# Who makes the sums of weight blocks in the gated layers' way down: VectorE, or an accumulating DMA issued by GpSimd

## The reference, cut to what matters

```
def swiglu(x, w_in, w_out):
    gate, up = jnp.split(x @ w_in, 2, axis=-1)     # w_in: 1024 x 5632
    return (jax.nn.silu(gate) * up) @ w_out        # w_out: 2816 x 1024
x = x + 0.5 * rms_norm(swiglu(rms_norm(x, ln_ffn1_pre[l]), w_ffn1_in[l], w_ffn1_out[l]), ln_ffn1_post[l])
```

## Time and profile before

| what | us |
|---|---|
| median of 3 runs | 2791.99 (2789.7 to 2792.78) |
| the profiled execution's own time | 2794.04 |
| its span, first to last instruction | 2792.3 |
| PE busy | 2722.2 (97% of the span) |
| DVE busy | 2006.4 (72%) |
| ACT busy | 1407.1 (50%) |
| POOL busy | 58.2 (2%) |
| mean of what the DMA engines moved | 94 GB/s |

### The profile page before, as it was taken

The page is one execution under the profiler, slowest core; times in us unless marked ns, Lnnn a source line. Parts: engine busy times, 40 slices in busy tenths (PEclk is TensorE's granted clock), DMA queues, the critical chain, the costliest instruction groups (busy, mean ns, idle before and its releaser), DMA issues. The chain is left out here.

```text
span 2792.3 us, 51093 instructions
## 1 busy us (share of the span) xinstructions
PE 2722.2 (97%) x21196; PEld 2405.1 (86%) x21196; DVE 2006.4 (72%) x2795; ACT 1407.1 (50%) x2154; POOL 58.2 (2%) x45
## 2 busy tenths in 40 slices
PE   8999999999999999999999999999999998999998
PEld 7999888778999878999888777999888877888877
DVE  7888855676887876887856777788785369666674
ACT  4445544555544455544545555444556367444442
POOL 1000000001000001000000000100000000000000
PEclk9999999999999999999999999999999999999999
DMA  4334311103233231334122103133422111322243
GB/s 150 107 106 174 104 49 61 40 4 121 85 106 132 110 136 46 99 106 176 62 86 76 55 3 114 61 107 106 159 96 101 62 51 35 114 82 94 96 166 106
DMA packets 72806, 261.26 MB, mean 94 GB/s; under 512 B 7864, under 2 KB 8888, under 8 KB 72576
## 3 DMA queue, kind: packets, MB, share of 16 engines
q1 hardware_dynamic: 72576, 257.99, 26.9%
HBM read 255.86 MB, written 2.10 MB: 92 GB/s over the span
## 5 line engine op out<-in xcount | busy, mean ns | idle before, releaser
L261 PE MATMUL ps<-h_hi,w_space 128*128 128x512 f32 (+1 forms) x2624 | 697.5, 351 | 3.4 <-DVE h_lo L367 3.4
L261 PEld LDWEIGHTS ps<-h_hi,w_space 128*128 128x128 f32 x2624 | 462.6, 190 | 70.5 <-DVE h_lo L367 4.2
L271 PE MATMUL ps<-w_space 128*128 128x512 f32 x2064 | 480.2, 391 | 1.7 <-DVE w_space L249 0.9
L249 DVE TENSOR_TENSOR w_space<-w_raw,w_space 128x1024 fp32r<-128x1024 f32 x252 | 307.1, 1230 | 214.6 <-ACT w_space L241 214.5
L261 PE MATMUL ps<-h_lo,w_space 128*128 128x512 f32 (+1 forms) x1312 | 457.4, 349 | 0.0
L271 PEld LDWEIGHTS ps<-w_space 128*128 128x128 f32 x2064 | 385.3, 188 | 81.8 <-DVE w_space L249 1.7
L848 PE MATMUL ps<-h_hi,w_space 128*128 128x256 f32 x2432 | 450.8, 283 | 0.0
L848 PEld LDWEIGHTS ps<-h_hi,w_space 128*128 128x128 f32 x2432 | 385.2, 192 | 0.2
L848 PE MATMUL ps<-h_lo,w_space 128*128 128x256 f32 x1216 | 344.3, 283 | 0.0
L241 ACT CAST w_space<-w_raw 128x1024 fp32r<-128x1024 f32 x252 | 261.0, 1047 | 159.5 <-PE ps L261 97.3
L261 PEld LDWEIGHTS ps<-h_lo,w_space 128*128 128x128 f32 x1312 | 249.4, 190 | 29.8 <-issue 0.5
(11 more groups left out here) (532 smaller groups left out, 3978.3 us busy)
## 6 DMA issues: line engine op xcount, KB each, us to landing
w_raw<-in_w_ffn_in SPq DMA_DIRECT2D x176, 512.0 KB, 3.4
w_raw<-in_w_in SPq DMA_DIRECT2D x64, 512.0 KB, 3.4
w_raw<-in_w_ffn_out SPq DMA_DIRECT2D x56, 512.0 KB, 3.5
w_raw<-in_w_up SPq DMA_DIRECT2D x44, 512.0 KB, 3.4
w_raw<-in_w_down SPq DMA_DIRECT2D x34, 512.0 KB, 4.1
row_blocks<-in_w_ffn_out SPq DMA_DIRECT2D x8, 2048.0 KB, 11.6
w_raw<-in_w_out SPq DMA_DIRECT2D x24, 512.0 KB, 4.3
w_raw<-in_w_ple_gate SPq DMA_DIRECT2D x16, 512.0 KB, 3.8
```

The lines of the kernel that those rows point to most:

```text
L249: nc.vector.tensor_tensor(self.shaped(unit, self.lo(n)), self.whole_of(unit), self.shaped(unit, self.hi(n)).bitcast(F32), ALU.subtract).th ...
L261: m = nc.tensor.matmul(c.ps[:, bank, t], part[:, cols], moving[:, k, t], start=(opens and k == 0 and i == 0), stop=(k == KD - 1 and i == 2 ...
L271: m = nc.tensor.matmul(c.ps[:, bank + half, :], x, part[:, half * S:(half + 1) * S], start=(first and i == 0), stop=(final and i == 2), sk ...
```

## The change

The four weight sums of each group are no longer made by DVE. POOL issues for each one a DMA that reads a block of `w_out` from HBM and adds it to the block that lies in SBUF (`accum_op=ALU.add`). Since such a DMA only adds, the signs of the scheme are turned: m5 uses b11+b12, m6 b11+b12+b22, m7 b12+b22, m4 b11+b12+b22+b21, and the activation sums and the joins of the products take the opposite signs where needed (same number, shapes and places of DVE instructions). ACT waits for the DMA's semaphore in place of DVE's. Beside that, in the attention that follows, five semaphores become two (`cos_done` and `sin_done` are `halves_done`; `summed` and `inverted` are `shared`), with the same waits in other counts.

```diff
     def waiting(self, name, g):
         def wait(eng):
             if name in SUMMED_WEIGHTS:
-                self.wait_rested(eng, "weights", name, g)
+                self.wait_weights(eng, name, g)
...
+    def wait_weights(self, eng, name, g):
+        eng.wait_ge(self.c.blocks_summed[g], 16 * (1 + len(SUMMED_WEIGHTS) * self.stage + SUMMED_WEIGHTS.index(name)))
...
     def vector_down(self, dve, nc, early, last):
         for k in range(4, UNITS):
             self.collect(dve, nc, k)
-            if k + 2 < UNITS and DOWN_STEPS[k + 2][0] in SUMMED_WEIGHTS:
-                self.weight_sum(dve, nc, *DOWN_STEPS[k + 2])
...
-    def weight_sum(self, dve, nc, name, g):
...
-        if name == "m5":
-            self.wait_blocks(dve, g)
-            nc.vector.tensor_tensor(b11, b12, b11, ALU.subtract).then_inc(done, 1)
...
+    def weight_sums(self, pool, nc):
+
+        for i, name in enumerate(SUMMED_WEIGHTS):
+            part, rows, half = {"m5": ("m1", 0, 1), "m6": ("m1", 2, 1), "m7": ("m7", 2, 1), "m4": ("m1", 2, 0)}[name]
+            before = {"m5": "m1", "m6": "m5", "m4": "m6"}.get(name)
+            for g in range(2):
+                if i:
+                    self.wait_weights(pool, SUMMED_WEIGHTS[i - 1], g)
+                else:
+                    self.wait_blocks(pool, g)
+                if before:
+                    pool.wait_ge(self.c.W.lo_ready, self.down.d0 + STEP_OF[before, g] + 1)
+                pool.dma_start(self.block_weights(part, g), self.w_blocks[g][:, rows:rows + 2, half * S:(half + 1) * S],
+                               accum_op=ALU.add).then_inc(self.c.blocks_summed[g], 16)
...
-            nc.vector.tensor_tensor(total, a21, a22, ALU.add).then_inc(done, 1)
+            nc.vector.tensor_tensor(total, a21, a22, ALU.subtract).then_inc(done, 1)
...
-            nc.vector.tensor_tensor(total, total, a11, ALU.subtract).then_inc(done, 1)
+            nc.vector.tensor_tensor(total, a11, total, ALU.subtract).then_inc(done, 1)
...
-            self.add_sums(dve, nc, "m1", "m5")
+            self.add_sums(dve, nc, "m5", "m5", "m1", ALU.subtract)
...
-            self.join(dve, nc, "m5", "m7")
+            self.join(dve, nc, "m5", "m7", ALU.subtract)
...
                 ffn2.gpsimd(pool, nc)
+                ffn2.weight_sums(pool, nc)
                 if ffn1 is not None:
                     ffn1.gpsimd(pool, nc)
+                    ffn1.weight_sums(pool, nc)
                     attention.gpsimd(pool, nc)
```

More of the change, by code:

```diff
@@ L646, in __init__ @@
             rested += self.collected(k)
-            rested += [("weights",) + step for step in DOWN_STEPS[k + 2:k + 3] if step[0] in SUMMED_WEIGHTS]
             rested += [("acts",) + step for step in DOWN_STEPS[k + 1:k + 2] if step[0] in SUMMED_ACTS]
@@ L1226, in take_out, with add_sums, join @@
                                 ALU.subtract).then_inc(c.seven_rested, 1)
[L1228 to L1232, removed]
+    def add_sums(self, dve, nc, to, first, second, op):
+        nc.vector.tensor_tensor(self.block_sum(to), self.block_sum(first), self.block_sum(second), op).then_inc(self.c.seven_rested, 1)
+    def join(self, dve, nc, name, product, op=ALU.add):
         banks = self.block_banks(name)
-        nc.vector.tensor_tensor(banks, banks, self.block_sum(product), ALU.add).then_inc(self.c.seven_rested, 1)
+        nc.vector.tensor_tensor(banks, banks, self.block_sum(product), op).then_inc(self.c.seven_rested, 1)
     def collect(self, dve, nc, k):
@@ L1242, in collect @@
             self.wait_rested(dve, "out", "m5")
-            self.add_sums(dve, nc, "m1", "m5")
+            self.add_sums(dve, nc, "m5", "m5", "m1", ALU.subtract)
         if k == STEP_OF["m2", 1]:
             self.wait_rested(dve, "out", "m6")
-            self.add_sums(dve, nc, "m1", "m6")
+            self.add_sums(dve, nc, "m6", "m1", "m6", ALU.subtract)
         if k == STEP_OF["m2", 1] + 1:
@@ L1249, in collect @@
             self.wait_rested(dve, "out", "m7")
-            self.add_sums(dve, nc, "m6", "m7")
+            self.add_sums(dve, nc, "m7", "m6", "m7", ALU.add)
         if k == STEP_OF["row", TAKEN["m7"]] + 4:
@@ L1669, in __init__ @@
         self.loaded, self.consts, self.ones_set = st.sem("loaded"), st.sem("consts"), st.sem("ones_set")
-        self.sinks_ready, self.turned, self.cos_done = st.sem("sinks_ready"), st.sem("partner_turned"), st.sem("cos_done")
-        self.sin_done, self.roped = st.sem("sin_done"), st.sem("roped")
+        self.sinks_ready, self.turned, self.halves_done = st.sem("sinks_ready"), st.sem("partner_turned"), st.sem("halves_done")
+        self.roped = st.sem("roped")
         self.v_turned, self.v_copied = st.sem("v_turned"), st.sem("v_copied")
@@ L1676, in __init__ @@
         self.exps, self.sink_exps, self.pv_done = st.sem("exps"), st.sem("sink_exps"), st.sem("pv_done")
-        self.summed, self.inverted, self.normed = st.sem("summed"), st.sem("inverted"), st.sem("normed")
+        self.shared, self.normed = st.sem("shared"), st.sem("normed")
         self.transposed, self.out_copied = st.sem("transposed"), st.sem("out_copied")
@@ L1798, in exponents @@
         if h >= 2:
-            act.wait_ge(self.summed, h - 1)
+            act.wait_ge(self.shared, 2 * (h - 2) + 1)
         nc.scalar.activation(self.sink_exp[:, h % 2, :, 0], self.neg_top[:, h % 2, :].bitcast(F32), ACT.Exp, scale=self.SCALE,
@@ L1850, in rotate @@
         nc.vector.stream_shuffle(self.turned_sin[:, :], u, ROPE_PARTNER).then_inc(self.turned, 1)
-        nc.vector.tensor_tensor(self.rotated[:, :], u, c.rope[:, 0, :], ALU.mult).then_inc(self.cos_done, 1)
+        nc.vector.tensor_tensor(self.rotated[:, :], u, c.rope[:, 0, :], ALU.mult).then_inc(self.halves_done, 1)
         dve.wait_ge(self.turned, i + 1)
         nc.vector.tensor_tensor(self.turned_sin[:, :], self.turned_sin[:, :], c.rope[:, 1, :],
-                                ALU.mult).then_inc(self.sin_done, 1)
-        dve.wait_ge(self.cos_done, i + 1)
-        dve.wait_ge(self.sin_done, i + 1)
+                                ALU.mult).then_inc(self.halves_done, 1)
+        dve.wait_ge(self.halves_done, 2 * (i + 1))
         nc.vector.tensor_tensor(u, self.rotated[:, :], self.turned_sin[:, :], ALU.add).then_inc(self.roped, 1)
@@ L1896, in normalise @@
         nc.vector.tensor_tensor(self.share[:, h % 2, :, :], o[:, :, DH:DH + 1], self.sink_exp[:, h % 2, :, :],
[L1897 to L1900, removed]
+                                ALU.add).then_inc(self.shared, 1)
+        dve.wait_ge(self.shared, 2 * h + 1)
+        nc.vector.reciprocal(self.share[:, h % 2, :, :], self.share[:, h % 2, :, :]).then_inc(self.shared, 1)
+        dve.wait_ge(self.shared, 2 * h + 2)
         if t:
@@ L4113, in _ @@
                 ffn.gpsimd(pool, nc)
+                ffn.weight_sums(pool, nc)
                 attention.gpsimd(pool, nc)
@@ L4352, in signals @@
     c.rec_loaded = sem("rec_loaded")
+    c.blocks_summed = [sem(f"blocks_summed{g}") for g in range(2)]
     c.made, c.reduced, c.sines, c.table_chain, c.table_loaded = (sem(n) for n in ("made", "reduced", "sines", "table_chain", "table_loaded"))
```

8 lines of the change are left out of this document (removed).

## The result

The median after is 2801.21 us (7 runs, 2797.46 to 2802.96), beside 2791.99 us before: a ratio of 1.0029, with a 95% interval of 1.0020 to 1.0038. The change makes the kernel about 8 us slower. The time lies in the predicted range (2786 to 2808), but only because that range had been widened for rival 1. The likeliest case, no change, did not happen; rival 1, an accumulating DMA that is too slow for m5, did, at a smaller size than it was priced.

The account below looks back on a forecast made before the run. PE's own pace was taken to bound the ways down. Terms of 0 + 0 left the profiled 2794.0 us, given as 2792.0 on the median's scale; range 2786 to 2808, to hold 8 in 10.

Parts of the forecast that it names:

- The likeliest case: Whole run: time stays 2792.0 us, own range 2788 to 2797; chance of staying within 0.2%: 0.65.
- rival 1: m5 of group 0: accumulating DMA slow, ACT waits and holds PE; 2802 us at T = 10, 2815 at 11.6; chance 0.23.
- What bounds the kernel now: Four ways down: PE's own pace bounds, 5.44 us a step, busy 436.70 of 438.00 us; DVE runs ahead.
- What goes: Ways down: DVE loses 32 instructions, 38.9 us of busy time, worth 0 to 1.3 us; taken as 0.
- What comes: Ways down: POOL issues 32 sums; T taken as 5 us, ends 3.5 and 11.6; nothing late, stall 0.
- T: Time from DVE having the rest of the block's last user until the sum has landed; taken as 5 us.
- How much T is allowed: m5 of group 0: 6.9, 9.8, 9.7 and 8.8 us in the four ways down before PE's m1 is late.
- What the DMAs collide with: Sums add 16.8 MB of reading; beside full DMA engines in the second way down T reaches 7.2 us; price 0.
- Rival 2: Ways down: POOL can't write descriptors beside a busy DVE; T = 7.4, 2792.5 us, or 2822 needing a gap; chance 0.05.
- Rival 3: Ways down: DVE's 38.9 us count after all, faster than 2786.4; rows give 2790.7; chance of gain over 0.2%: 0.07.
- Rival 4: POOL's order holds sums back, each waiting for the one before in its group; still 2792 us; no chance given.

Follow-up runs that it names:

- the second execution: The changed kernel itself run once more beside the kernel before, with nothing further changed: 2800.04 us, ratio 1.0027.
- the kernel with m5 in b12: Against the changed kernel, m5's sum is made in b12's place and issued when its block lands; a fifth DMA restores b12's copy for m7: 2805.51 us, ratio 1.0038.

## Why the prediction came out as it did

- **What bounds the kernel now** held. PE's pace of 5.44 us a step stayed, with or without sums on DVE, and DVE's 38.9 us were worth nothing, as with m5 back on DVE.
- **What goes** held: 0.
- **What comes** is the step that failed, in one term: T was taken as 5 us and is 8.2 to 10.8. Its parts can now be named. The 3.5 us was counted from issue to landing on SP's queue, but the wait begins at DVE's rest: POOL's wake takes 0.65 us, its DMA instruction 0.85, and a plain DMA from POOL then lands so that ACT starts 4.85 us later, 6.35 together. Accumulating adds 1.9 (first way down, 8.2), of which 0.5 is in POOL's instruction (1.33 for 0.85). The estimate had 1.24 for it. In the other three ways down the same DMA, plain, already takes 8.0 to 9.1, beside the loads that are under way.
- **How much T is allowed** held: 6.9, 9.8, 9.7 and 8.8 us gave each stall within 0.1 us, once the rest of m1 is put where it stood. The copy "was m1" behind m5's high part on ACT was the place. m6 of both groups, m7 and m4 were never late: allowed times of 8.5 us and more covered T there, even with m5 late: for m6 of group 0 it was 6.4 to 7.3 us.
- **What the DMAs collide with** failed in size: T at most 7.2 in the full stretches, measured 10.4 to 10.8. There I read the share 0.25 at 262 to 265 as room for the first sum, but the sum is issued at 260, and 256 to 262 is full, from the blocks' own loads, in the kernel after (1.02) as in the one before (1.01 and 1.02). The same rows 11 were read for DVE: it was busy for 1.30 of the 3.00 us at 259 to 262, not without a gap. A price was put on the sum's bytes, none on its standing beside a backlog. Two kernels show it: issued 2.4 us earlier in the first way down it lands no earlier, and with idle engines at the issue T is 6.7. The sums then fill the engines, 1.11 busy at 206 GB/s at 265 to 268, where loads move 418 at 1.02. The plain rows' loads pay as well: their median from issue to landing is 4.8 us in the kernel after and 3.5 before, but PE waited for none of them.
- **Rival 1** is what happened. It "decides from T = 6.9 on", which it did. At T = 10 it had 4.8 us for m5, about right (6.2 measured with T over 10 in three of four), and 5.6 us for m6, which did not come, since m6's T was 6.4 to 7.3 and not 10. Its chance, 0.23, was too low: the nearest row was a load on another queue, with no second read, into idle engines, and I took the sum close to it, although the other end, 11.6 us, was the row of a DMA among full engines, which is what the sums met.
- **Rival 2** did not happen. POOL's 32 DMA instructions took 1194 to 1333 ns each, 1.19 to 1.21 us both where DVE did nothing meanwhile (918.56, 1327.80) and where it was busy throughout (937.68, 1347.00). It is POOL's arithmetic that collides with DVE, not its DMAs. **Rival 3** did not happen. **Rival 4** did not either: POOL's order held no sum back so far that PE waited.

What stays open: the medians say 7 to 9 us, the stalls explain 6.2 to 6.8 of one execution. In the second execution the lower clock adds 1.4. The rest lies within the interval, and no further place was found. How much of T under full engines is queueing in each engine and how much is memory was not told apart. Of the 11 us that the kernel with m5 in b12 lost, its seven stops of PE at blocks explain 6.9 (2.8 before m1, 4.1 before m6) and the two at row 6 2.0. No version beat the kernel before: with PE busy 436.7 of 438 us there is nothing that a freed DVE could give.

## What to carry to other kernels

Before work moves from an engine that is not the bound to a DMA, compare two times: how long after the last reader of the buffer the consumer needs the result, and the whole way through the DMA (wake, the issuing instruction, landing), taken in the stretch where it is issued and beside the loads that are under way there. Look also at what stands behind the waiting instruction in its engine's order: here it was a copy for PE, and 0.7 to 2.4 us of lateness went straight to the end. An engine with slack and a result ahead of time need no relief.

## What the runs showed of the hardware that was not expected

- An accumulating DMA of 512 KB from POOL takes 3.15 us of all 16 engines where a plain one takes 1.6, and twice the packets (272 against 144 each). It lands after 7.6 us, the plain one from POOL after 4.6.
- POOL's DMA instruction itself is busy 1.20 us for an accumulating DMA, 0.73 for a plain one.
- A DMA of 512 KB issued into a backlog can land no earlier for being issued 2.4 us earlier (once, in the first way down; in another the same 2.4 us brought 2.1).
- A POOL add on SBUF stretches a two-input DVE instruction that it meets from 1.23 to 3.43 us and from 0.69 to 2.88.
- Six of eight stops of PE, 2.06 to 4.00 us long, were followed by a clock at its lower level (0.50) for some microseconds, and this made a loss of 20.5 us into one of 32.5. In the profiled execution of the changed kernel none of the four was, the longest 2.25 us; in its second one the stop of 3.16 us was, and cost 1.4 us more.
